# Two attention branches of a hybrid block: keys first and rotary scores from stacked halves in A, values on two halves of the array in B

## What is computed

```
# A: multi-head latent attention, 4 heads, 128 + 64 query/key dims, 128 value dims
q  = rmsnorm(c_q) @ w_uq;   kv = rmsnorm(c_kv) @ w_ukv
q_nope, q_rope = q[..., :128], q[..., 128:]          # per head
k_nope, v      = kv[..., :128], kv[..., 128:]
q_rope, k_rope = rope_2d(q_rope), rope_2d(k_rope)    # one k_rope for all heads
s = (q_nope @ k_nope.T + q_rope @ k_rope.T) * scale;  y = softmax(s) @ v
# B: grouped-query attention, 8 heads of 64 dims over 2 key/value heads,
#    a window of +-128 tokens plus the context, a sink logit per head
```

## Time and profile before

| | |
|---|---|
| time, median of 3 runs | 3169.16 us (3163.76 to 3171.29) |
| the profiled execution's own time | 3180.8 us |
| its span, first to last instruction | 3179.1 us |
| TensorE busy | 2950.7 us (93%) |
| TensorE clock granted, mean | 0.975 of full |
| VectorE, ScalarE busy | 1497.2 us, 1253.3 us |
| attention of A, layer 0 and layer 1, first score to last gate slice | about 532 to 663 us, 2242 to 2345 us |
| attention of B, layer 0 and layer 1 | about 768 to 949 us, 2429 to 2551 us |

### The profile page before, as it was taken

One profiled execution on the slowest core, in us unless ns is written; L12 is line 12 of the kernel. 1 busy time (PEld: TensorE's weight loads), 2 busy tenths in 40 slices (PEclk: granted clock), 3 DMA queues, 4 the chain that ended last, 5 costly groups with the idle time before them and its releaser, 6 DMA issues.

```text
span 3179.1 us, 37822 instructions
## 1 busy us (share of the span) xinstructions
PE 2950.7 (93%) x15104; PEld 2317.1 (73%) x15104; DVE 1497.2 (47%) x2318; ACT 1253.3 (39%) x2175; POOL 160.3 (5%) x182
## 2 busy tenths in 40 slices
PE   5998999999999989899999989998998899889998
PEld 4877785577668768788888868776456576678886
DVE  4267742345444434564344443873236545444344
ACT  4344333334553443544233344443334544342222
POOL 0022300000000000000000000230000000000000
PEclk8999998999999999999999999999899999999999
DMA  5222240022113123243333222223021030322332
GB/s 196 67 93 92 85 139 30 21 97 74 61 43 113 62 103 102 73 129 117 107 116 110 80 94 73 80 86 120 7 84 50 19 116 27 136 78 95 99 94 92
DMA packets 83960, 274.75 MB, mean 86 GB/s; under 512 B 9424, under 2 KB 9680, under 8 KB 82768
## 3 DMA queue, kind: packets, MB, share of 16 engines
q1 hardware_dynamic: 74896, 229.84, 22.0%
q0 software_dynamic: 8896, 42.55, 4.0%
HBM read 246.12 MB, written 26.22 MB: 86 GB/s over the span
## 4 chain that ended last, share of the span: by engine, by line
PE 78%; DVE 9%; ACT 7%; issue 3%; DMA 2%; POOL 0%; SPq 0%; DVEq 0%; ACTq 0%
PE slot L646 76%; PE slot L1063 2%; ACT tmp L1250 1%; DVE rowmax L1942 1%; ACT SS L1475 1%; DVE wl L1600 1%; DMA SS<-g_kept 1%; DMA raw<-w_merge_dram 1%; ACT PT_B L1461 1%; ACT Hh L1252 1%; DVE ada_prod L1976 1%; ACT ada_prod L1503 1%; ACT wh L1159 1%; DVE XS L1819 0%; DVE state L1858 0%
## 5 line engine op out<-in xcount | busy, mean ns | idle before, releaser
L646 PE MATMUL slot<-Hh,wh 128*128 128x512 f32 (+1 forms) x2368 | 871.8, 369 | 49.2 <-DVE Hl L1647 20.5
L646 PE MATMUL slot<-Hh,wl 128*128 128x512 f32 (+1 forms) x2368 | 838.3, 355 | 0.0
L646 PE MATMUL slot<-Hl,wh 128*128 128x512 f32 (+1 forms) x2368 | 837.8, 355 | 0.0
L646 PEld LDWEIGHTS slot<-Hh,wh 128*128 128x128 f32 x2368 | 453.2, 192 | 124.2 <-issue 31.9
L646 PEld LDWEIGHTS slot<-Hh,wl 128*128 128x128 f32 x2368 | 452.2, 191 | 63.6
L646 PEld LDWEIGHTS slot<-Hl,wh 128*128 128x128 f32 x2368 | 453.8, 192 | 59.4 <-issue 5.5
L1600 DVE TENSOR_TENSOR wl<-raw,wh 128x1024 fp32r<-128x1024 f32 (+1 forms) x208 | 227.7, 1095 | 237.2 <-ACT wh L1159 230.3
L646 PE MATMUL slot<-Uh,wh 128*128 128x512 f32 (+1 forms) x768 | 272.0, 354 | 2.5 <-DVE Ul L2018 2.5
L1942 DVE TENSOR_REDUCE rowmax<-slot 128x1 f32<-128x768 f32 (+3 forms) x160 | 123.3, 770 | 316.7 <-PE slot L646 315.9
L646 PE MATMUL slot<-Ul,wh 128*128 128x512 f32 (+1 forms) x768 | 272.0, 354 | 0.0
L646 PE MATMUL slot<-Uh,wl 128*128 128x512 f32 (+1 forms) x768 | 271.6, 354 | 0.0
(11 more groups left out here) (247 smaller groups left out, 4055.0 us busy)
## 6 DMA issues: line engine op xcount, KB each, us to landing
raw<-w_dram SPq DMA_DIRECT2D x204, 512.0 KB, 3.5
raw<-w_gate_dram SPq DMA_DIRECT2D x64, 512.0 KB, 3.5
ada_g_raw<-ada_dram POOLq DMA_DIRECT2D x48, 512.0 KB, 3.9
ada_g_raw<-ada_dram SPq DMA_DIRECT2D x32, 512.0 KB, 3.7
raw<-w_merge_dram SPq DMA_DIRECT2D x64, 256.0 KB, 2.7
g_kept<-logits_out SPq DMA_DIRECT2D x32, 384.0 KB, 2.3
SS<-g_kept SPq DMA_DIRECT2D x32, 384.0 KB, 3.3
ada_first<-ada_dram SPq DMA_DIRECT2D x8, 1024.0 KB, 18.3
```

Source lines behind the costliest of these rows:

```text
L646: return pe.matmul(dst, lhsT, rhs, start=start, stop=stop)
```

## The change

A: the latent for keys and values is projected before the one for queries; its norm, the keys and the values come first, then the rotary queries, then the four heads' queries, with the two rotations placed between them. The rotated key `KR` is split into `KR_HIGH` and `KR_LOW` (fp32r), and each head's rotary query is stacked as high part on its own 64 partitions and low part on the other 64 of `Yh`. A rotary score block is then two full 128-row `fp32r` matmuls. DVE and ACT gain the splits (`a_high`, `a_low`). The last head's copy is waited for behind the first tile's scores.

B: each value product is issued as two matmuls of 256 columns, even heads to PSUM partitions 0 to 63 and odd heads to 64 to 127; the output is written out in one piece.

```diff
-    "A": [("cq", 0), ("cq", 1), ("ckv", 0)],
+    "A": [("ckv", 0), ("cq", 0), ("cq", 1)],
...
+        KR_HIGH, KR_LOW = rows("KR_high", R_S + 12, 1, f32r)[:, 0, :], rows("KR_low", R_S + 11, 1, f32r)[:, 0, :]
+        ROTATED_A = [slot[3][:, bank * SEQ:(bank + 1) * SEQ] for bank in range(2)]
...
-                src = values_at[0:B_HD, 0:tile["width"]].rearrange("p (a o s) -> p o a s", o=2, s=P)
-                return [(dst[odd * B_HD:(odd + 1) * B_HD, 2 * g:2 * g + 2, n * P:(n + 1) * P], src[:, odd, :, :]) for odd in range(2)]
+                return [(dst[:, 2 * g:2 * g + 2, n * P:(n + 1) * P], values_at[:, 0:2 * P].rearrange("p (a s) -> p a s", s=P))]
```

PE's `branch_a`. The loops over keys and values in the middle are unchanged; the loop over `order` is the one that stood ahead of them:

```diff
-                chain_begins()
+                for k in (0, 2, 3):
+                    pe.wait_ge(*slots.last(k))
                 chain_rotate(0, misc, A_ROPE)
-                pe.wait_ge(normed.sem, w.next(normed, 2))
-                order = [(None, h) for h in range(A_HEADS)] + [("rope", j) for j in range(2)]
...
                 pe.wait_ge(normed.sem, w.next(normed))
                 for h in range(A_HEADS):
...
-                pe.wait_ge(copied.sem, w.next(copied, COPIES["A"]))
-                for j in range(2):
-                    chain_rotate(j, QR[:, j, :])
-                pe.wait_ge(roped.sem, w.next(roped, 4))
+                pe.wait_ge(normed.sem, w.next(normed, 2))
+                order = [("rope", j) for j in range(2)] + [(None, h) for h in range(A_HEADS)]
...
+                    if n in (2, 3):
+
+                        pe.wait_ge(copied.sem, w.next(copied, N_PROJ["A"] + A_HEADS + NB + 1 if n == 2 else 1))
+                        chain_rotate(3 - n, QR[:, n - 2, :])
+                pe.wait_ge(copied.sem, w.next(copied, A_HEADS - 1))
+                pe.wait_ge(a_low.sem, w.next(a_low, 3))
+                pe.wait_ge(*slots.last(1))
+
+            def last_query_copied():
+
+                pe.wait_ge(copied.sem, w.next(copied))
                 chain_over(("c0", "c2", ("rotated", 0), ("rotated", 1)))
```

PE's `attention`:

```diff
-                                    part = slice((h % 2) * A_ROPE, (h % 2 + 1) * A_ROPE)
                                     mm(out_s[:, lo:hi], QY[:, h, qs_], KN[h][:, lo:hi], start=True, stop=False)
-                                    last = mm(out_s[:, lo:hi], QR[part, h // 2, qs_], KR[part, lo:hi], start=False, stop=True)
+                                    mm(out_s[:, lo:hi], Yh[:, h, qs_], KR_HIGH[:, lo:hi], start=False, stop=False)
+                                    last = mm(out_s[:, lo:hi], Yh[:, h, qs_], KR_LOW[:, lo:hi], start=False, stop=True)
...
+                        if branch == "A" and i == 0:
+                            last_query_copied()
...
-                                last = mm(values_at[0:B_HD, 0:tile["width"]], VB[:, m, g * B_HD:(g + 1) * B_HD], pt, **flags)
+                                by_half = pt.rearrange("p (a o s) -> p o a s", o=2, s=P)
+                                for odd in range(2):
+                                    strip = slice(odd * B_HD, (odd + 1) * B_HD)
+                                    last = mm(values_at[strip, 0:2 * P].rearrange("p (a s) -> p a s", s=P),
+                                              VB[:, m, g * B_HD:(g + 1) * B_HD], by_half[:, odd, :, :], **flags)
```

ACT's `branch_a` copies keys and values first, then the two rows of `QR`, then the heads' queries in this loop:

```diff
+                for h in range(A_HEADS):
+                    act.wait_ge(proj_done.sem, w.next(proj_done))
+                    act.activation(QY[:, h, 0:nq], slot[2 * (h % 2)][:, 0:nq], ACT.Copy).then_inc(copied.sem, 1)
+                    if h == 0:
+                        act.wait_ge(roped.sem, w.next(roped, 2 + (6 if layer else 0)))
+                        act.activation(KR_HIGH, KR, ACT.Copy).then_inc(a_high.sem, 1)
+                    elif h < 3:
+                        j = h - 1
+                        act.wait_ge(roped.sem, w.next(roped))
+                        for odd in range(2):
+                            part = slice(odd * A_ROPE, (odd + 1) * A_ROPE)
+                            ins = act.activation(Yh[part, 2 * j + odd, 0:nq], QR[part, j, 0:nq], ACT.Copy)
+                        ins.then_inc(a_high.sem, 1)
```

DVE's `branch_a` takes the key latent's norm first, then the query latent's two, then the key's rotation, and behind it:

```diff
                 for j in range(2):
-                    rope(QR[:, j, :], slot[1][:, j * SEQ:(j + 1) * SEQ], ROT["A"])
+                    rope(QR[:, j, :], ROTATED_A[1 - j], ROT["A"])
                     dve.wait_ge(roped.sem, w.next(roped))
+                    if j == 0:
+                        dve.wait_ge(a_high.sem, w.next(a_high))
+                        dve.tensor_tensor(KR_LOW, KR, KR_HIGH.bitcast(f32), ALU.subtract).then_inc(a_low.sem, 1)
+                for j in range(2):
+                    dve.wait_ge(a_high.sem, w.next(a_high))
+                    for odd in range(2):
+                        part, other = slice(odd * A_ROPE, (odd + 1) * A_ROPE), slice((1 - odd) * A_ROPE, (2 - odd) * A_ROPE)
+                        high = Yh[part, 2 * j + odd, 0:nq].bitcast(f32)
+                        ins = dve.tensor_tensor(Yh[other, 2 * j + odd, 0:nq], QR[part, j, 0:nq], high, ALU.subtract)
+                    ins.then_inc(a_low.sem, 1)
```

More of the change, by code:

```diff
@@ L284, in build @@
         masks_in = sig("masks_in", unit=16)
+        a_high, a_low = sig("a_high"), sig("a_low")
         split_high, split_low, masks_split = sig("split_high"), sig("split_low"), sig("masks_split")
@@ L836, in chain_rotate @@
                 pe.wait_ge(*slots.next(("rotated", bank), rot_read))
[L837 removed]
+                mm(ROTATED_A[bank][0:parts, :], rot_t[0:parts, 0:parts], src[0:parts, 0:SEQ]).then_inc(rot_done.sem, 1)
             def decay_logits(h):
@@ L990, in branch_a @@
                        w_ukv[:, A_HEADS:2 * A_HEADS, :]).then_inc(proj_done.sem, 1)
-                pe.wait_ge(copied.sem, w.next(copied, COPIES["A"]))
-                for j in range(2):
-                    chain_rotate(j, QR[:, j, :])
-                pe.wait_ge(roped.sem, w.next(roped, 4))
+                pe.wait_ge(normed.sem, w.next(normed, 2))
+                order = [("rope", j) for j in range(2)] + [(None, h) for h in range(A_HEADS)]
+                for n, (kind, h) in enumerate(order):
+                    where = 2 * (n % 2)
+                    pe.wait_ge(*slots.next(f"c{where}", copied))
+                    block_at = h if kind is None else A_HEADS + h
+                    for k in range(2):
+                        for lo, hi in chunks(nq):
+                            last = mm(slot[where][:, lo:hi], w_uq[:, k, block_at * P:(block_at + 1) * P], XS[:, k, lo:hi],
+                                      start=k == 0, stop=k == 1)
+                    last.then_inc(proj_done.sem, 1)
+                    if n in (2, 3):
[6 more added lines that the diff above has]
+                pe.wait_ge(copied.sem, w.next(copied))
                 chain_over(("c0", "c2", ("rotated", 0), ("rotated", 1)))
@@ L1281, in copy_out @@
                     elif branch == "A":
-                        if n == 2:
-                            act.wait_ge(sum_done.sem, w.next(sum_done))
                         act.activation(SQ["A"][n % 2][:, 0:nn], s[:, 0:nn], ACT.Square).then_inc(squared.sem, 1)
-                        act.activation(XS[:, n, 0:nn], s[:, 0:nn], ACT.Copy).then_inc(copied.sem, 1)
+                        act.activation(XS[:, j if kind == "cq" else 2, 0:nn], s[:, 0:nn], ACT.Copy).then_inc(copied.sem, 1)
                     elif branch == "B":
@@ L1332, in project @@
                         act.activation(dst, slot[beside][:, 0:T], ACT.Copy).then_inc(copied.sem, 1)
+                    elif branch == "A" and kind == "ckv":
+                        rsqrt(slot[3], T, A_KV_RANK, RSTD["A"][1], 1)
                     elif branch == "D":
@@ L1430, in branch_c, with branch_a @@
                     whole_out(layer, i, i + 1 < WHOLE_GATES[layer])
[L1432 to L1437, removed]
+            def branch_a(layer, nq):
                 for h in range(A_HEADS):
@@ L1444, in branch_a @@
                     act.activation(va[:, n * SEQ:(n + 1) * SEQ], slot[2 * (n % 2)][:, 0:SEQ], ACT.Copy).then_inc(copied.sem, 1)
+                act.wait_ge(normed.sem, w.next(normed, 3))
+                for j in range(2):
+                    act.wait_ge(proj_done.sem, w.next(proj_done))
+                    act.activation(QR[:, j, 0:nq], slot[2 * j][:, 0:nq], ACT.Copy).then_inc(copied.sem, 1)
+                for h in range(A_HEADS):
+                    act.wait_ge(proj_done.sem, w.next(proj_done))
+                    act.activation(QY[:, h, 0:nq], slot[2 * (h % 2)][:, 0:nq], ACT.Copy).then_inc(copied.sem, 1)
[9 more added lines that the diff above has]
+                        ins.then_inc(a_high.sem, 1)
             def attention(branch, layer):
@@ L1569, in _ @@
                     if b == "A":
-                        branch_a(nq)
+                        branch_a(layer, nq)
                     if b != "C":
@@ L1912, in branch_a @@
                 dve.wait_ge(rstd_ready.sem, w.next(rstd_ready))
```

(10 more changed lines are left out.)

10 lines of the change are left out of this document (4 added, 6 removed).

## The result

The changed kernel takes 3080.6 us (median of 4 runs, 3071.7 to 3082.1), the one before 3170.2 (4 runs, 3163.8 to 3173.5): a ratio of 0.9714, 95% interval 0.9696 to 0.9732. The forecast was 3078, with a range of 3052 to 3114. The profiled execution of after has a span of 3070.0 us, where that of before has 3179.1.

The account below looks back on a forecast made before the run. TensorE, busy 93% of the span, was taken as the bound. Scores 36, waits 7, clock 17 and values 31 sum to 91 us, so 3169 - 91 = 3078 us, range 3052 to 3114.

Parts of the forecast that it names:

- A, the scores: A's score tiles: split 128-row matmuls replace 64-row f32 ones, 41 us less new idle of 5, so 36 us saved.
- The chain rival: Tiles of A and B shrink only to DVE's and ACT's chain; A gives 25, B 18, total 3102 us; chance 12%.
- A, the waits: Ahead of A's attention: three old PE waits (5.8 us a layer) give way to one new wait; 7 us saved.
- the list of waits: Ahead of A's attention: norm, copy and rotation waits go; only a wait for low parts is new, 2.0 and 2.1 us.
- A, the clock: Behind A's first scores: the long half-speed stretches, 20.5 us lost, shrink to brief dips; 17 us saved.
- one brief dip per layer: Behind A's new wait: 3.4 us at half level in each layer, 1.7 us lost each time.
- The sign I gave: Start of A's attention: mean PE clock of 0.8 or more over the first 24 us.
- B, the values: B's value matmuls: two column halves overlap, 34 us less PE work, 85% of it showing, plus output; 31 us saved.
- the four strips: Modulation matmuls on four 32-column strips, 0.12 us a record against 0.43 alone; taken to show B's halves overlap fully.
- the 85%: In B, the share of the 34 us less PE work expected to show as time: 29 us.
- Two of the signs: In A: PE's idle passing 5 us a layer, and PEclk staying at 0.5 for over 10 us.
- A in layer 1 some 33 us shorter: A's attention in layer 1, from first score to last, was to shorten by some 33 us.

Follow-up runs that it names:

- e5_order_only: The changed kernel without c0 in the handover after the first A scores, but with the old 64-row f32 rotary scores and no split copies; 3104.9 us, ratio 0.9798.
- e1_no_c0: The changed kernel with slot c0 taken out of the handover (`chain_over`) after the first A scores; 3069.8 us, ratio 0.9670 to the kernel before.
- e3_b_alone: The kernel before with only B's change: values in two column halves, output written in one piece; 3132.5 us, ratio 0.9880.
- the last three kernels: e5_order_only, e7_long_wait and e8_old_scores_wait, which vary TensorE's stop ahead of A's first scores and the work behind it; 3104.9, 3079.1 and 3126.6 us.
- e8_old_scores_wait: e5_order_only with eleven useless VectorE additions that make TensorE stop ahead of A's first scores; 3126.6 us, ratio 0.9855.
- e7_long_wait: e1_no_c0 with six useless VectorE additions that make TensorE stop longer ahead of A's first scores; 3079.1 us, ratio 0.9716.

## Why the prediction was right, and where it was not

The total came out as forecast, but in part by luck: two of its four terms were too high (waits and clock, by 7 us together) and two too low (scores and values, by 11), and the mistakes nearly cancelled.

- **A, the scores: 36 forecast.** The cleanest reading is e5_order_only against e1_no_c0, both at full clock behind the first scores (e1_no_c0 has one later low stretch of 3.4 us in layer 0): A's stretches are 130.3 and 92.5 us against 108.9 and 71.3, 42.6 us less in all. By ratios it is (0.9798 - 0.9670) x 3171 = 41 us of time, on top of the 4 us of first stops that only e1_no_c0 has; the two intervals together leave some 8 us either way. Two parts of the sum were mis-sized: a tile takes 2.00 and not 2.1 us, and the new idle is smaller than the 2.5 us a layer that I charged. Over A's stretches PE idles 5.3 and 1.5 us in e1_no_c0, against 3.1 and 1.5 in e5_order_only: 2.2 us in all. DVE and ACT did keep up: behind the first scores PE is busy 18.25 of 19 and 23.97 of 24 us in e1_no_c0. The chain rival falls.
- **A, the waits: 7 forecast.** The stretch ahead of the first scores is 4.1 + 4.4 = 8.5 us shorter, and the new wait is 2.04 and 1.98 us where 2.0 and 2.1 were forecast. In layer 1 VectorE runs the forecast chain without a gap; in layer 0 it stands 1.17 us in it for ScalarE's last high part. The step that failed is the list of waits: it ended at `a_low`. The handover after the first tile adds 2 x 2.31, so the term is 3.9 us. The diff shows it: `chain_over` moved behind a score that takes the slot it names.
- **A, the clock: 17 forecast.** 7 + 10 us at the half level remain of 17 + 24, 2.3 of them standing, so (41 - 14.7) / 2 = 13 us were gained in this pair of profiles. With e3_b_alone's 17 + 7 as the old state it would have been (24 - 14.7) / 2 = 5: the term is right in kind, and its size hangs on the execution. The step that failed is "one brief dip per layer": layer 0 of after has two such dips and layer 1 one of 10.2 us. In layer 0 the first is the forecast one and the second stands behind the second stop; without that stop, e1_no_c0 has none at all. The forecast reason, that the 64-row work was what made the dips long, is borne out in tendency and with a condition, by the last three kernels: the 64-row work goes with long dips, but only behind a stop. The sign I gave, PEclk of 0.8 or more over the first 24 us, was just missed in layer 1 (0.79).
- **B, the values: 31 forecast.** The stretches are 20.9 + 14.2 = 35.1 us shorter, B alone is worth 40 by time with an interval of 31 to 45. The overlap is full, as read from the four strips: 74.6 - 38.9 = 35.7 us of PE. The step that failed is the 85%: B's idle PE did not grow but fell. Over the stretches of the table it is 178.35 - 167.21 = 11.1 and 116.10 - 101.69 = 14.4 us before, 157.53 - 148.57 = 9.0 and 101.91 - 88.42 = 13.5 after. I had also split it evenly over the layers; layer 0 has the larger share.

Sum by the measured terms: 42.6 + 3.9 + 13 + 35.1 = 94.6 us, beside 94.9 in the stretches and 89.7 in the medians. By the estimate from the Trainium skill's page TensorE: Matmul & The Clock Gate, Part 3, with its factor of 2.38 for three column tiles, the values' gain would have been 26 us; the trace disagrees for two halves, with 35.7.

Two of the signs by which I had said that I would be wrong did show, though the total held. PE's idle in A was to stay under 5 us a layer: in after it is 113.11 - 105.55 = 7.6 us in layer 0 (3.8 in layer 1), 2.3 of it the second stop. And PEclk was not to stay at 0.5 for over 10 us: in layer 1 it did, for 10.2. "A in layer 1 some 33 us shorter" came out at 26.0.

Open: what sets the length of a single low stretch, 24 us in layer 1 of before, 11 in e8_old_scores_wait behind a longer stop. The kernel before has a second, short wait of 0.7 us some microseconds ahead of it, at the rotations. That wait does not explain the 24: e3_b_alone has it too, 0.69 us at the same place, and stayed low for 7.

## What to carry to other kernels

When a handover of buffers is moved, ask who holds each buffer at the new place: here one name too many cost 11 us, 4.6 of them standing and the rest, by the difference between the runs, in the clock. Price a stop of TensorE with the work that follows it; two of 2 us close together (the changed kernel, 3080) cost as much as one of 6.4 (e7_long_wait, 3079). Matmuls whose outputs lie on different column halves should be issued alternately: side by side, the pair takes the time of one.

## What was not expected of the hardware

- Around two stops of 2.0 and 2.3 us with 3 to 4 us of work between, TensorE was at the half level for 3.4, 7 or 10 us (eight layer starts in four runs). In six of them the clock fell before the second stop, yet the stop of 2.0 us alone left no fall in four starts, and one of 6.4 only 3.4 to 3.8 us behind it.
- The same 64-row work behind the same stop of 3.37 us ran at the half level for 24 us in one profile and 7 in another (before and e3_b_alone, layer 1), which makes 7.9 us of A's stretch.
- Matmuls on different column halves overlap even when they are issued as two runs: 57.0 us for 320 records, between the 38.9 side by side and the 74.6 of the full-width form.
- The 64-row f32 matmuls ran at the full clock from the start of A where no stop stood ahead (e5_order_only, 1.00 over 19 and 24 us), and at 0.55 over 19 us behind 3.7 us of standing.
